# Triangular inverses on all four quarters of TensorE, with operands on swapped halves

## The chip, the cores and the metric

One core of one Trainium2 chip. The metric is device time in microseconds (us) of one execution, median over runs. Engines: PE (TensorE matmul) and PEld (its weight loads), DVE (VectorE), ACT (ScalarE), POOL (GpSimd), SP (SyncE, which issues DMAs here). TensorE's clock is granted at 2.4 GHz (1.00 in the profile) or 1.2 GHz (0.50).

## The reference, cut to what matters

Two stacked models; the change touches only the two chunked scans of the first. The GDN scan solves, per chunk of 64 tokens and head, with a unit lower triangular matrix:

```python
a_mat = jnp.where(strict, bc[..., :, None] * kk * gamma, 0.0) + jnp.eye(C)
u = lax.linalg.triangular_solve(a_mat, bc[..., None] * vc, left_side=True, lower=True)
w = lax.linalg.triangular_solve(a_mat, (bc * jnp.exp(G))[..., None] * kc, left_side=True, lower=True)
...
S = S * jnp.exp(g_last) + einsum(k * jnp.exp(g_last - G), u - w @ S)     # step over 12 chunks
```

The RWKV-7 scan goes token by token, 8 heads of 64, forward and backward; the kernel does it in chunks of 128 tokens:

```python
sa = einsum('bhvk,bhk->bhv', S, -kk_t)
S = S * w_t + sa * (kk_t * a_t) + v_t * k_t
y_t = einsum('bhvk,bhk->bhv', S, r_t)
```

Sequence: 256 context tokens and 512 others, width 1024, all in float32. In both scans the kernel needs the inverse (transposed, TT) of I + A for a strictly triangular 128x128 matrix A per head and chunk of 128.

## The kernel before, in words

The program is 17 stages, one after the other. In each, every engine has its own instruction list, written by generator functions that `in_turn` interleaves round by round; the order on an engine is the order in which the generators yield. Engines wait for each other by semaphores (`wait_ge(*P.at(name))` for the value that `up(name)` gave). There is no planner: the order is fixed by the code.

**PSUM banks.** The eight banks are a ring (`P.bank`, a helper that calls `P.own`): each use takes the next bank and makes PE wait until the bank's previous user is marked "free" (its reader is done). In the GDN scan the ring has 7 banks, since bank 7 belongs to the ada_w products (L551), which run between the scan's own work; in the RWKV scan it has 8.

**The inverse** (`Inverse`, L931 to L1051) works on four heads at once. A 128x128 matrix per head is split in two diagonal 64x64 blocks, one on partitions 0 to 63 and one on 64 to 127, and one off-diagonal block. Tile `TTm` holds `Tm` (the inverse so far) and `TD` (its transpose). ACT copies the diagonal blocks to `AD` and the other to `OFF` (`ac_in`, L1034, L1035). DVE makes `TD = I - AD * mask0` (L990, L992); PE transposes it to PSUM (`Ttr`, L958) and DVE copies that to `Tm` (L995). Then five levels s = 1 to 5 double the size of the solved blocks:

- POOL makes the masked `MT` for the level (L1018, L1023);
- PE: Y = MT by Tm (L949, 8 matmuls of 64x64), ACT copies it to SBUF (L1042);
- PE: the *level product* TY = TD by Y and YT = Y by TD (L949, 16 matmuls), both in one bank;
- DVE subtracts both from TTm in one instruction (L1002), or, at level 5, in three (L1005, two of L1009, which write TT).

At the end Y6 = OFF by Tm (L975), an ACT copy (L1046), U (L981), and an ACT copy into TT (L1049). In every diagonal product the operands and the output lie on the same 64 partitions, so that two of the array's four 64x64 quarters are in use. Each float32 matmul is two records in the trace, one behind the other in PE's list.

**The GDN scan** (`GdnScan`) has six steps, each with both directions d = 0 and 1 side by side. In the rounds of a step PE does: Ttr, WS (L1204), ada_w; Y1, vn (L1212), ada_w; level 1, o (L104) and dS (L1226), ada_w; Y2, qk, ada_w; level 2, gG (L1170); Y3; level 3, gB (L1176); Y4, kk (L1181); level 4; Y5; level 5; Y6; U. The matrix AT of the next step is made by DVE in SBUF during the step. The ada_w weights stream in by DMA, 2 MB at a time into two slots; each is used by two L551 groups.

**The RWKV scan** (`RwkvScan`) has 12 units u, six blocks of 128 tokens forward and six backward; block b is ORDER[u // 6][u % 6], with ORDER = ([0, 1, 2, 3, 4, 5], [1, 0, 5, 4, 3, 2]). Two inverses q = 0, 1 (four heads each) run side by side. PE's order in a unit: AT, BT and, for b >= 2, Qb and Qk (all L1567, two banks each), X of the chain of unit u-1 (L1586, L1589), SA (L1597), Ttr, r_w of the preparation of u+1 (L1723), y of the chain, Y1, r_a (L1728), rS (L104), level 1, and so on; the preparation's transposes (L1736) stand before Y4. DVE's: BT's copy (L1641), TD of both q, the copies of Qb and Qk (L1651), then chain, inverses and preparation in turn. ACT's: AD and OFF of q = 0, AD and OFF of q = 1, X's copy (L1701), SA's copy, and so on.

## Time and profile before

| | us |
|---|---|
| median of 3 runs | 4419.53 |
| lowest, highest run | 4417.85, 4431.77 |
| span of the profiled execution (its own time beside that is not given) | 4426.6 |
| busy in the span: PE, PEld | 3814.4, 2105.2 |
| busy: DVE, POOL, ACT | 2195.7, 1302.2, 878.9 |

The span is from the first to the last instruction. "Busy" is the union of an engine's instructions; matmuls are pipelined and their ends modelled, so PE's busy time is an upper bound of its work. The two scans take 320 us and 535 us of the span. In a timeline row the columns are: start, duration, engine, line, operation, output <- inputs, shapes, count of merged instructions, and in brackets the idle time of the engine before it and what ended it. The duration of a merged row includes the last matmul's pipeline (0.22 us at full clock); how long a row holds the engine is the distance to the next row's start.

### The profile page before, as it was taken

Reading aid. Unit: us, or ns where it says so; the run is one execution under the profiler, and the core shown is the slowest. Engines: PE = TensorE matmul, PEld = TensorE weight load, DVE = VectorE, ACT = ScalarE, POOL = GpSimd, SP = SyncE. Lnnn points to the kernel's source line nnn. Section 1 sums busy time; section 2 is a strip of 40 time slices with the busy share of each in tenths; the row PEclk is TensorE's granted clock in tenths of the full one; section 3 lists DMA queues with packets and bytes.
Section 4 is the critical chain, followed back from the end, with each engine's and each line's share of the span. In section 5 each row is a group of like instructions: output and inputs, shape, how many; then the busy total and the mean of one; then the engine's idle time right before and its main releaser. Section 6 shows DMA issues by size and latency. Waiting matters only on the chain.

```text
span 4426.6 us, 51891 instructions
## 1 busy us (share of the span) xinstructions
PE 3814.4 (86%) x21059; PEld 2105.2 (48%) x21059; DVE 2195.7 (50%) x4428; ACT 878.9 (20%) x1998; POOL 1302.2 (29%) x1372
## 2 busy tenths in 40 slices
PE   7988898888899677777777777779999999989999
PEld 4556665888874322222222222355555444544444
DVE  4845434666544677677577454353332016533320
ACT  1422122333321111111111111221111011521100
POOL 1033301333310277777777777300000000000000
PEclk8999998999899799999999999989999999999999
DMA  4155520000021499999999999711111111012221
GB/s 157 56 190 211 198 70 8 2 2 2 2 73 60 154 409 409 409 409 409 409 409 409 409 400 409 290 35 57 57 39 57 52 50 63 1 39 76 76 71 71
DMA packets 240812, 743.00 MB, mean 168 GB/s; under 512 B 20214, under 2 KB 66561, under 8 KB 231104
## 3 DMA queue, kind: packets, MB, share of 16 engines
q0 software_dynamic: 150992, 549.82, 31.4%
q1 hardware_dynamic: 89008, 187.77, 12.0%
q8 instruction: 168, 2.75, 0.3%
q10 hardware_dynamic: 576, 2.10, 0.1%
q14 instruction: 68, 0.56, 0.0%
HBM read 737.52 MB, written 2.10 MB: 167 GB/s over the span
## 4 chain that ended last, share of the span: by engine, by line
PE 58%; DMA 18%; DVE 13%; POOL 5%; ACT 3%; issue 3%; DVEq 0%; ACTq 0%; POOLq 0%
PE bank L104 34%; DMA wring<-in_peer_down,idxs 11%; PE bank L2466 9%; DMA row<-in_peer_up,idxs 5%; PE bank L949 3%; DVE junk L2375 3%; POOL row L2360 2%; POOL wring L2353 2%; PE bank L2447 2%; DMA wring<-in_ada_w 1%; PE bank L1567 1%; PE bank L551 1%; DVE TTm L1002 1%; DMA row<-in_peer_down,idxs 1%; PE bank L1597 1%
## 5 line engine op out<-in xcount | busy, mean ns | idle before, releaser
L2447 PE MATMUL bank<-row,dg 128*128 128x512 f32 x2048 | 998.3, 618 | 334.3 <-DMA row<-in_peer_up,idxs 214.5
L2447 PEld LDWEIGHTS bank<-row,dg 128*128 128x128 f32 x2048 | 361.6, 193 | 970.6 <-issue 499.4
L104 PE MATMUL bank<-h2T,wring 128*128 128x512 f32 (+1 forms) x2112 | 759.6, 523 | 0.0
L2375 DVE CUSTOM_DVE_ANT_0 junk<-wring,bank 128x1024 f32<-128x1024 f32 x410 | 500.6, 1221 | 328.8 <-DMA wring<-in_peer_down,idxs 307.0
L104 PEld LDWEIGHTS bank<-h2T,wring 128*128 128x128 f32 x2112 | 402.7, 191 | 355.5 <-issue 337.1
L2360 POOL DMA_INDIRECT row<-in_peer_up,idxs x512 | 491.4, 960 | 175.9 <-issue 126.4
L2353 POOL DMA_INDIRECT wring<-in_peer_down,idxs x410 | 391.5, 955 | 146.7 <-issue 83.5
L2466 PE MATMUL bank<-wring,gT 128*128 128x512 f32 x880 | 383.2, 598 | 8.6 <-DVE gT L2864 8.6
L2427 ACT ACTIVATE dg<-consts,cf 128x128 f32<-128x128 f32 x512 | 192.5, 397 | 691.6 <-PE bank L2447 691.3
L2853 DVE TENSOR_SCALAR cv<-pad,fp 128x769 f32<-128x769 f32 (+1 forms) x88 | 54.1, 615 | 509.4 <-ACT pad L2819 509.4
L104 PE MATMUL bank<-hT,wring 128*128 128x256 f32 (+1 forms) x864 | 286.5, 492 | 3.7 <-ACT sq L768 3.0
L2466 PEld LDWEIGHTS bank<-wring,gT 128*128 128x128 f32 x880 | 168.5, 192 | 221.1 <-issue 221.1
L104 PEld LDWEIGHTS bank<-hT,wring 128*128 128x128 f32 x864 | 165.8, 193 | 119.8 <-issue 102.3
L2484 DVE TENSOR_TENSOR tmp<-bank,gr 128x512 f32<-128x512 f32 x28 | 19.3, 691 | 380.8 <-PE bank L2466 345.5
L2900 POOL DMA_DIRECT2D rope<-in_rope x1 | 0.6, 556 | 701.9 <-ACT h2T L2581 701.9
L1023 POOL TENSOR_TENSOR MT<-AD,consts 128x256 f32<-128x256 f32 x144 | 116.1, 825 | 171.8 <-PE bank L949 171.3
L2375 DVE CUSTOM_DVE_ANT_0 junk<-row,bank 128x1024 f32<-128x1024 f32 x102 | 124.5, 1221 | 80.7 <-DMA row<-in_peer_down,idxs 75.3
L104 PE MATMUL bank<-wring,h2T 128*128 128x512 f32 x352 | 156.1, 600 | 3.2 <-ACT h2T L2581 2.3
L949 PE MATMUL bank<-TTm,MT 64*64 64x64 f32 x2880 | 115.6, 227 | 41.2 <-DVE TTm L1002 38.7
L949 PEld LDWEIGHTS bank<-TTm,MT 64*64 64x64 f32 x2880 | 102.0, 139 | 75.2 <-issue 41.2
L1042 ACT ACTIVATE Y<-bank 128x256 f32<-128x256 f32 x180 | 68.2, 382 | 330.7 <-PE bank L949 327.8
L949 PE MATMUL bank<-Y,TTm 64*64 64x64 f32 x2880 | 119.5, 222 | 2.9 <-DVE eG L1256 1.3
(545 smaller groups left out, 4710.9 us busy)
## 6 DMA issues: line engine op xcount, KB each, us to landing
wring<-in_ada_w SPq DMA_DIRECT2D x36, 2048.0 KB, 8.6
wring<-in_ffn_w_up SPq DMA_DIRECT2D x44, 1024.0 KB, 7.7
wring<-in_ffn_w_down SPq DMA_DIRECT2D x8, 2048.0 KB, 8.1
wring<-in_w_in SPq DMA_DIRECT2D x7, 2048.0 KB, 8.2
wring<-in_peer_w_query SPq DMA_DIRECT2D x4, 2048.0 KB, 8.0
row<-in_peer_up,idxs POOLq DMA_INDIRECT x512, 18.2
wring<-in_peer_down,idxs POOLq DMA_INDIRECT x410, 18.0
wring<-in_ffn_w_down SPq DMA_DIRECT2D x4, 1536.0 KB, 6.7
```

Source lines behind the costliest of these rows:

```text
L104: ins = e.matmul(out, l, r, start=(start and n == 0), stop=(stop and n == len(pairs) - 1))
L551: ins = e.matmul(k[32 * j:32 * j + 32, :], P.sc[g // 3 > 0][:, c, :], wb[:, c % 2, j * 512:(j + 1) * 512], start=(c == 0), stop=(c == 7))
L949: ins = e.matmul(k[a, h * 64:(h + 1) * 64], l[a, h, :], r[a, h, :], start=True, stop=True)
L1023: e.tensor_tensor(w["MT"][(s + 1) % 2], w["AD"], self.mask(s + 1), MUL).then_inc(*G.up("MT", u, s + 1))
L1042: e.activation(w["Y"], q4(P.ps("Y", u, s)), ACT.Copy).then_inc(*A.up("free", "Y", u, s))
L2353: e.indirect_dma_start(self.rd[r], None, down, bass.IndirectOffsetOnAxis(ap=idu[:, b, j % 128:j % 128 + 1], axis=0)).then_inc(*self.Ld[r]. ...
L2360: e.indirect_dma_start(self.ru[r], None, up, bass.IndirectOffsetOnAxis(ap=idu[:, b, u % 128:u % 128 + 1], axis=0)).then_inc(*self.Lu[r].up ...
L2375: e.tensor_tensor_reduce(junk, self.rd[j % 10], P.pairs[b % 2], 1.0, 0.0, MUL, ADD, self.dots[:, b % 2, x:x + 1]).then_inc(*V.up("pg_dot", j))
L2427: e.activation(self.dg[u % 4], P.ident, ACT.Copy, scale=self.cf[:, b % 2, x:x + 1]).then_inc(*A.up("pg_scaled", u))
L2447: ins = e.matmul(ks[half], self.dg[u % 4], self.ru[u % 10][:, half * 512:half * 512 + 512], start=(x == 0), stop=(x == 127))
L2466: ins = pe.e.matmul(ks[b], oT[:, k0 + c, off + b * 128:off + (b + 1) * 128], wb[:, c, :], start=(k0 + c == 0), stop=(k0 + c == kc - 1))
L2853: e.tensor_scalar(cc, p[:, s0:s0 + m - 1], w(0), w(3), MUL, ADD).then_inc(*V.up())
```

## The change

- **Banks.** PSUM is declared as four pairs of banks. Each `Inverse` gets a number q and owns pair q: bank A = 2q and bank B = 2q + 1. TY goes to A and YT to B, in columns 0 to 255; Ttr and Y go to B, columns 256 to 511; U goes to A. DVE reads TY and YT in one instruction over both banks (`both`). In the RWKV scan AT goes to A of both inverses as well.
- **The ring** is what is left: banks 4 to 7 in the RWKV scan (ring 4 instead of 8), banks 4 to 6 in the GDN scan (3 instead of 7).
- **Halves.** AD, MT and Tm lie on the other half of the partitions than TD and Y. So Ttr and TY go from rows of one half to columns of the other, Y is made from the swapped halves, and the new `level` function issues TY and YT alternately, so that four matmuls in a row use the four quarters.
- **TD.** DVE reads the source itself instead of AD, in two multiplications of 64 partitions (since the halves are not swapped there), then the subtraction. In the GDN scan the source is AT in SBUF, and DVE waits for AT only; in the RWKV scan it is AT in PSUM, and DVE waits until ACT has made AD.
- **Order.** ACT copies AD of both inverses first and OFF afterwards, once DVE has made TD (`ac_off`). In the RWKV scan DVE makes TD of both inverses before it copies BT.

```diff
-            self.banks = [bank(n, 512) for n in range(4)]
-            self.pairs = [bank(n, 1024) for n in (4, 6)]
-            self.banks += [p[:, s:s + 512] for p in self.pairs for s in (0, 512)]
+            twos = [bank(n, 1024) for n in (0, 2, 4, 6)]
+            self.banks = [p[:, s:s + 512] for p in twos for s in (0, 512)]
+            self.twos = [p.rearrange("p (a i) -> p a i", a=2) for p in twos]
+            self.pairs = twos[2:]
...
-        return self.own(pe, n, *user)
+        return self.own(pe, self.low + n, *user)
...
+    def level(self, pe, u, s):
+        P, e, w = self.P, pe.e, self.w
+        ty, yt = P.own(pe, self.A, "TY", u, s), P.own(pe, self.B, "YT", u, s)
         for h in range(4):
-            for a in (slice(0, 64), slice(64, 128)):
-                ins = e.matmul(k[a, h * 64:(h + 1) * 64], l[a, h, :], r[a, h, :], start=True, stop=True)
-        return ins
+            for a, b in self.halves:
+                e.matmul(ty[b, h * 64:(h + 1) * 64], w["TD"][a, h, :], w["Y"][a, h, :], start=True, stop=True)
+                ins = e.matmul(yt[a, h * 64:(h + 1) * 64], w["Y"][a, h, :], w["TD"][a, h, :], start=True, stop=True)
+        ins.then_inc(*self.st.T.up("TYT", u, s))
...
-            self.pairs(e, k, w["MT"][s % 2], w["Tm"]).then_inc(*T_.up("Yps", u, s))
+            for h in range(4):
+                for a, b in self.halves:
+                    ins = e.matmul(k[a, h * 64:(h + 1) * 64], w["MT"][s % 2][b, h, :], w["Tm"][b, h, :], start=True, stop=True)
+            ins.then_inc(*T_.up("Yps", u, s))
...
-            ins = e.matmul(k[hi, h * 64:(h + 1) * 64], w["OFF"][lo, h, :], w["Tm"][lo, h, :], start=True, stop=True)
+            ins = e.matmul(k[hi, h * 64:(h + 1) * 64], w["OFF"][hi, h, :], w["Tm"][hi, h, :], start=True, stop=True)
...
-        dv.wait_ge(*P.at("AD", u))
+        dv.wait_ge(*P.at(*given))
         if over:
             dv.wait_ge(*P.at(*over))
-        e.tensor_tensor(w["TD"], w["AD"], self.mask(0), MUL).then_inc(*V.up())
+        m0 = self.mask(0)
+        for a, _ in self.halves:
+            e.tensor_tensor(w["TD"][a], src[a, :, a], m0[a], MUL).then_inc(*V.up())
...
-        for a in (slice(0, 64), slice(64, 128)):
-            e.activation(w["AD"][a], src[a, :, a], ACT.Copy).then_inc(*A.up("AD", u))
-        e.activation(w["OFF"][lo], src[lo, :, hi], ACT.Copy).then_inc(*A.up(*free))
+        for a, b in self.halves:
+            e.activation(w["AD"][b], src[a, :, a], ACT.Copy).then_inc(*A.up("AD", u))
+
+    def ac_off(self, ac, u, src, free, over):
+        P, e, w, A, lo, hi = self.P, ac.e, self.w, self.st.A, self.lo, self.hi
+        ac.wait_ge(*P.at("TT", u, 0))
+        if over:
+            ac.wait_ge(*P.at(*over))
+        e.activation(w["OFF"][hi], src[lo, :, hi], ACT.Copy).then_inc(*A.up(*free))
...
 class GdnScan: def pe
-        P.ring = 7
+        P.low, P.ring, P.turn = 4, 3, 0
 class GdnScan: def dv
-            invs = [self.inv[d].dv(dv, (step, d), ("Yps", (step - 1, d), 6) if step else None,
+            invs = [self.inv[d].dv(dv, (step, d), self.W[d]["AT"], ("AT", (step, d)), ("Yps", (step - 1, d), 6) if step else None,
                                    ("vn", (step - 1, d)) if step else None) for d in range(2)]
...
 class RwkvScan: def pe
+        P.low, P.ring, P.turn = 4, 4, 0
...
-                ks = [P.bank(pe, name, u, q) for q in range(2)]
+                ks = [P.own(pe, 2 * q, name, u, q) if name == "AT" else P.bank(pe, name, u, q) for q in range(2)]
 class RwkvScan: def dv
+            invs = [self.inv[u][q].dv(dv, ("r", u, q), v4(P.ps("AT", u, q)), ("AD", ("r", u, q)), ("Yps", ("r", u - 1, q), 6) if u else None,
+                                      ("SA", u - 2) if u >= 2 else None) for q in range(2)]
+            for g in invs:
+                next(g)
             dv.wait_ge(*P.at("BT", u))
             for q in range(2):
                 e.copy_predicated(res[q]["BT"], stri, v4(P.ps("BT", u, q))).then_inc(*V.up("free", "BT", u, q))
             V.mark("free", "BT", u)
-            invs = [self.inv[u][q].dv(dv, ("r", u, q), ("Yps", ("r", u - 1, q), 6) if u else None, ("SA", u - 2) if u >= 2 else None)
-                    for q in range(2)]
-            for g in invs:
-                next(g)
```

## Rows read from the trace of the kernel before

**Rows 1.** The page, the chain that ended last: share of the span by line.
```profile
PE bank L104 34%; DMA wring<-in_peer_down,idxs 11%; PE bank L2466 9%; DMA row<-in_peer_up,idxs 5%; PE bank L949 3%; DVE junk L2375 3%; POOL row L2360 2%; POOL wring L2353 2%; PE bank L2447 2%; DMA wring<-in_ada_w 1%; PE bank L1567 1%; PE bank L551 1%; DVE TTm L1002 1%; DMA row<-in_peer_down,idxs 1%; PE bank L1597 1%
```

**Rows 2.** Busy time by stretch (stretch, length, engines, clock, DMA): the two scans.
```profile
240.00:560.00 320.00, 264.16 (x4284) 193.94 (x4284) 165.56 (x444) 66.06 (x164) 118.96 (x120) 0.94 0.56 209
745.00:1280.00 535.00, 461.37 (x8391) 431.57 (x8390) 312.86 (x515) 179.41 (x380) 168.57 (x171) 0.91 0.01 4
```

**Rows 3.** Timeline of PE: 128x512 on the full array and on four column tiles.
```profile
206.80 13.90 PE L104 MATMUL bank<-wring,hT 128*128 128x512 f32 x32
...
420.69 1.06 PE L551 MATMUL bank<-wring,sc 128*32 128x512 f32 x8
```

**Rows 4.** Timelines of PE, DVE and ACT: end of RWKV unit 4, from level 4.
```profile
912.95 0.68 PE L949 MATMUL bank<-Y,TTm 64*64 64x64 f32 x16
...
914.98 0.68 PE L949 MATMUL bank<-TTm,MT 64*64 64x64 f32 x16
...
916.40 0.66 PE L949 MATMUL bank<-Y,TTm 64*64 64x64 f32 x16
...
918.82 0.68 PE L975 MATMUL bank<-TTm,OFF 64*64 64x64 f32 x8 [0.36 <-DVE TT L1009]
...
921.80 1.16 PE L1567 MATMUL bank<-al,be 64*128 64x128 f32 x16
...
914.14 0.69 DVE L1002 TENSOR_TENSOR TTm<-TTm,bank 128x512 f32<-128x512 f32 x1 [2.25 <-PE bank L949]
915.08 0.69 DVE L1002 TENSOR_TENSOR TTm<-TTm,bank 128x512 f32<-128x512 f32 x1 [0.24 <-PE bank L949]
917.56 0.41 DVE L1005 TENSOR_TENSOR TTm<-TTm,bank 64x256 f32<-64x256 f32 x1 [1.80 <-PE bank L949]
...
918.79 0.41 DVE L1005 TENSOR_TENSOR TTm<-TTm,bank 64x256 f32<-64x256 f32 x1
...
921.90 0.38 ACT L1049 ACTIVATE TT<-bank 64x256 f32<-64x256 f32 x1 [0.36 <-PE bank L981]
```

**Rows 5.** The same timelines: start of RWKV unit 4.
```profile
878.76 1.16 PE L1567 MATMUL bank<-al,be 64*128 64x128 f32 x16
...
881.54 1.06 PE L1567 MATMUL bank<-rho,ka 64*128 64x128 f32 x16
...
880.86 1.35 DVE L1641 COPY_PREDICATED BT<-consts,bank 128x512 f32<-128x512 uint32 x2 [3.91 <-PE bank L1567]
...
882.94 0.83 DVE L992 TENSOR_TENSOR TTm<-consts,TTm 128x256 f32<-128x256 f32 x1
...
885.02 1.33 DVE L1651 COPY_PREDICATED Qb<-consts,bank 128x512 f32<-128x512 uint32 x2
...
879.97 0.78 ACT L1034 ACTIVATE AD<-bank 64x256 f32<-64x256 f32 x2 [0.72 <-PE bank L1567]
```

**Rows 6.** Timelines of PE, DVE and ACT: GDN steps meet; a wait for DMA.
```profile
295.32 1.50 PE L551 MATMUL bank<-wring,sc 128*32 128x512 f32 x8 [2.42 <-DMA wring<-in_ada_w]
...
398.04 0.96 PE L981 MATMUL bank<-TT,Y 64*64 64x64 f32 x16
401.79 2.33 PE L958 MATMUL bank<-consts,TTm 64*64 64x64 f32 x32 [2.79 <-DVE TTm L992]
...
395.95 0.43 DVE L1009 TENSOR_TENSOR TT<-TTm,bank 64x256 f32<-64x256 f32 x1
...
399.56 0.85 ACT L1034 ACTIVATE AD<-AT 64x256 f32<-64x256 f32 x2
```

**Rows 7.** Busy time and granted clock by stretch.
```profile
402.00:408.00 6.00, 5.92 (x52) 5.34 (x54) 1.73 (x4) 0.00 (x0) 2.20 (x3) 0.50 0.47 201
518.00:521.00 3.00, 3.00 (x26) 2.88 (x25) 0.11 (x1) 0.00 (x0) 0.94 (x2) 0.50 0.59 240
437.00:441.00 4.00, 2.14 (x41) 1.97 (x40) 3.59 (x13) 1.07 (x3) 0.00 (x0) 1.00 0.88 369
805.00:818.00 13.00, 13.00 (x108) 11.98 (x109) 4.00 (x7) 3.80 (x6) 3.86 (x4) 0.50 0.00 0
1142.00:1162.00 20.00, 20.00 (x139) 19.08 (x138) 4.48 (x7) 3.90 (x6) 2.79 (x3) 0.51 0.01 2
```

More of the change, by code:

```diff
@@ L211, in __init__ @@
                 self.known, self.value = self.value, {}
[L212 removed]
+                self.holder, self.turn, self.ring, self.low, self.nw = [None] * 8, 0, 8, 0, {"pe": 0, "sy": 0}
                 for s in self.flags:
@@ L994, in dv @@
         dv.wait_ge(*P.at("Ttr", u))
-        e.tensor_copy(w["Tm"], q4(P.ps("Ttr", u))).then_inc(*V.up("free", "Ttr", u))
+        e.tensor_copy(w["Tm"], v4(P.ps("Ttr", u)[:, 256:512])).then_inc(*V.up("free", "Ttr", u))
         yield
@@ L999, in dv @@
             dv.wait_ge(*P.at("TYT", u, s))
[L1000 removed]
+            ps = self.both
             if s < 5:
[L1002 to L1003 removed]
+                tt = w["TTm"].rearrange("p a h i -> p a (h i)")
+                e.tensor_tensor(tt, tt, ps, SUB).then_inc(*V.up("TT", u, s))
             else:
[L1005 removed]
+                e.tensor_tensor(w["Tm"][hi], w["Tm"][hi], v4(ps[:, 0])[hi], SUB).then_inc(*V.up())
                 if over_tt:
                     dv.wait_ge(*P.at(*over_tt))
[L1008 to L1010 removed]
+                for a, _ in self.halves:
+                    e.tensor_tensor(w["TT"][a, :, a], w["TD"][a], v4(ps[:, 1])[a], SUB).then_inc(*V.up("TT", u, s))
+            for x in ("TY", "YT"):
+                V.mark("free", x, u, s)
             yield
@@ L1025, in po, with ac_in @@
             yield
-    def ac_in(self, ac, u, src, given, free, over):
-        P, e, w, A, lo, hi = self.P, ac.e, self.w, self.st.A, self.lo, self.hi
+    def ac_in(self, ac, u, src, given, over):
+        P, e, w, A = self.P, ac.e, self.w, self.st.A
         ac.wait_ge(*P.at(*given))
@@ L1041, in ac @@
             ac.wait_ge(*P.at("Yps", u, s))
-            e.activation(w["Y"], q4(P.ps("Y", u, s)), ACT.Copy).then_inc(*A.up("free", "Y", u, s))
+            e.activation(w["Y"], v4(P.ps("Y", u, s)[:, 256:512]), ACT.Copy).then_inc(*A.up("free", "Y", u, s))
             yield
@@ L1045, in ac @@
         ac.wait_ge(*P.at("Yps", u, 6))
-        e.activation(w["Y"][hi], q4(P.ps("Y", u, 6))[hi], ACT.Copy).then_inc(*A.up("free", "Y", u, 6))
+        e.activation(w["Y"][hi], v4(P.ps("Y", u, 6)[:, 256:512])[hi], ACT.Copy).then_inc(*A.up("free", "Y", u, 6))
         yield
@@ L1075, in __init__ @@
         P.top = top
-        self.inv = [Inverse(self, d, self.W[d]) for d in range(2)]
+        self.inv = [Inverse(self, d, self.W[d], d) for d in range(2)]
         self.og = P.ogdn.rearrange("p b (h e) -> p b h e", h=4)
@@ L1101, in pe @@
         in_turn(*[self.tail_pe(pe, 5, d) for d in range(2)])
-        P.ring = 8
+        P.low, P.ring = 0, 8
     def dv(self, dv):
@@ L1139, in ac @@
                 u = (step, d)
-                self.inv[d].ac_in(ac, u, self.W[d]["AT"], ("AT", u), ("AT_free", u), ("MT", (step - 1, d), 5) if step else None)
+                self.inv[d].ac_in(ac, u, self.W[d]["AT"], ("AT", u), ("MT", (step - 1, d), 5) if step else None)
+            for d in range(2):
+                u = (step, d)
+                self.inv[d].ac_off(ac, u, self.W[d]["AT"], ("AT_free", u), ("Yps", (step - 1, d), 6) if step else None)
             in_turn(*[self.inv[d].ac(ac, (step, d)) for d in range(2)],
@@ L1573, in pe @@
         in_turn(self.chain_pe(pe, 11))
+        P.low, P.ring = 0, 8
     def chain_pe(self, pe, u):
@@ L1689, in ac @@
             for q in range(2):
-                self.inv[u][q].ac_in(ac, ("r", u, q), v4(P.ps("AT", u, q)), ("AT", u), ("free", "AT", u, q),
-                                     ("MT", ("r", u - 1, q), 5) if u else None)
+                self.inv[u][q].ac_in(ac, ("r", u, q), v4(P.ps("AT", u, q)), ("AT", u), ("MT", ("r", u - 1, q), 5) if u else None)
+            for q in range(2):
+                self.inv[u][q].ac_off(ac, ("r", u, q), v4(P.ps("AT", u, q)), ("free", "AT", u, q),
+                                      ("Yps", ("r", u - 1, q), 6) if u else None)
             chain = self.chain_ac(ac, u - 1) if u else iter(())
```

35 lines of the change are left out of this document (13 added, 22 removed).

## The prediction

> **What bounds the kernel now.** I read four views in this order. The chain of waits says who sets the end: TensorE first, DMA second, and the line of the inverses' matmuls (L949) with 3% of the span [rows 1]. The two scans were then cut out by stretches [rows 2]: the GDN scan is 320 us of the span with PE busy 264, the RWKV scan 535 us with PE busy 461. All that the change touches lies in these 855 us, in which no other engine is busy for more than 60% of the time. The timelines of one RWKV unit (u=4) and of one GDN step show what the bound is at each place; in both, PE runs its queue in order and a wait at its head holds everything behind it.
>
> The profiled execution has a span of 4426.6 us; the runs are 4417.85 to 4431.77, median 4419.53, so it is 7.1 us (0.16%) above the median and inside the runs' spread. I work with differences and put them on the median.
>
> **Term 1: the level product.** Per level and inverse, TY and YT are 16 small matmuls, each two records. Before, they run as two groups of 16 records of 0.47 us, 0.93 us together, from the level product's start at 916.40 to DVE's start at 917.56 with 0.25 us of latency [rows 4]. Two tiles already overlap there: 16 records on two tiles show the same 0.68 us as 8 records on one tile in Y6 [rows 4]. Do four quarters overlap four ways? The nearest row is the ada_w matmul, which has four column tiles: 8 records of 128x512 let the next instruction start 0.99 us later, 124 ns each, where a full-array 128x512 takes 13.9/32 = 434 ns [rows 3]. That is 3.5 times, with each matmul's two records next to each other in the queue as here. So I take 0.47 us for a level product; the other end is 0.93, no gain. The Trainium skill ("TensorE: Matmul & The Clock Gate", Part 3, The mechanism) says that a weight load overlaps running matmuls only where the row group differs. Here TY and YT of one half share their rows; by the rule the level product would stay near 0.93 us. The ada_w row disagrees with it, since there all four tiles share every row and still run at once; it keeps a small chance.
>
> **Term 2: RWKV tail of a unit.** Levels 2 and 3 are held by DVE, which has the next unit's preparation between its subtractions; there a faster PE gains nothing. Level 4 on is free of it. Level 4 starts at 912.95 in both versions. With 0.47: the first TTm at 913.67 instead of 914.14; the second inverse's level product waits for its Y copy (913.45), its TTm can start at 914.28 instead of 915.08 (now behind DVE's first, 0.61). Y5 is 0.5 and 0.8 earlier, level 5 starts at 915.69 instead of 916.40, the last subtractions at 916.40 instead of 917.56 and, 1.23 later, 917.63 instead of 918.79 [rows 4]. Y6 follows 1.16 us earlier. Eleven units: -12.8. The last unit has no preparation, so levels 2 to 5 gain some 0.7 us each: -3.0. Sum **-15.8 us**.
>
> **Term 3: AT waits for U's copy.** AT(u+1) now goes into the inverses' own banks A, where U was last. Before, AT starts at 921.80, right behind U; ACT's copy of the second U is 921.90 to 922.28 [rows 4], so AT starts at about 922.4: +0.6 x 11 = **+6.6 us**.
>
> **Term 4: Qk waits for BT in a ring of four.** Banks 4 to 7 now serve everything else. BT takes two, Qb two, and Qk needs BT's two again, so PE stands until DVE has copied BT. And DVE now does the first two TD before BT. From AT's start (878.76 as zero) [rows 5]: ACT starts at 1.2 and needs 0.78 for the first AD pair; the second pair, no longer behind OFF, ends at 2.8. DVE reads the bank from 2.05: two half multiplications (0.41, 0.35 apart) to 2.9, the subtraction 0.83 as beside POOL now, to 3.75; the second inverse the same, to 5.1. BT's copies, 1.35, end at 6.5. Qk starts at 6.6, where it was at 881.54, or 2.8: 3.8 us later. X needs Qb's bank (its copy ends at 7.1) and starts behind Qk. Behind X stand SA, Ttr, r_w, Y1 and r_a, all PE-bound up to DVE's preparation, so nothing absorbs it. Bounds: 3.0 (subtractions at 0.42) to 4.2. It holds for units with b>=2, 8 of 12: **+30.4 us** (24 to 34). In units 1, 6 and 7 only ACT's X copy stands behind the second OFF, which waits for TD: +0.65 x 3 = **+2 us**.
>
> **Term 5: GDN, TD without ACT.** Before, PE stands 2.79 us in front of Ttr at 401.79, for TTm (L992): U's copies, then AD, then two DVE instructions [rows 6]. The source AT is in SBUF and long ready, and DVE is done with the step's last TT at 396.4, so with the new source TD is made while PE still works on Y6 and U. Ttr follows U at once. Such a gap stands in front of steps 1 to 5, 2.7 us each: -13.5; step 0 saves ACT's copies, about 1.2. These gaps also cost clock. After that of 2.79 us the granted clock is 0.50 (1.2 GHz) over 402 to 408, with PE busy 5.92 of 6.0; an idle stretch of 1.86 us at 437 leaves it at 1.00 (2.4 GHz) [rows 7]. Two other steps have the same gap and a shorter half-clock stretch behind it, as over 518 to 521; with theirs I estimate 14 us at half clock, half of it lost: -7. Sum **-22 us** (-12 if the clock stays as it is, -25).
>
> **Term 6: GDN levels.** Levels 1, 2 and 4 are followed at once by work on which the step's chain depends; level 3 is held by DVE (gm, eG), level 5 mostly by the ada_w DMA (a wait as at 295.32) [rows 6]. 0.47 x 2 x 3 in six steps is 17; with two level 5 that are free and some loss to DVE **-17 us** (0 without the four-way overlap, -22 at best). The ring of three costs little here: I followed each use to the one three before it, and only gB of the second direction waits for eG, in a place that DVE holds anyway.
>
> **Term 7: the clock in the RWKV stalls.** Term 4 puts an idle PE of 3.8 us into eight units, longer than the gaps after which the clock fell. And where it falls in front of SA and Ttr it stays down long: PE is busy all of 805 to 818 and of 1142 to 1162 at 0.50 [rows 7]. If a fall follows in 8 of 10 cases and lasts 10 us with PE on the path for most of it, half is lost at worst: I take 4 us x 6.5 = **+26 us** (0 to +70).
>
> The other edits cost nothing on the path: in the GDN scan DVE's second multiplication lies in its idle time behind U, OFF's later copy has until Y6, the swap of halves in AD and MT changes only addresses, and Y6 and U, which share rows now, may lose 0.2 us where they interleave.
>
> **Sum.** -15.8 + 6.6 + 30.4 + 2 - 22 - 17 + 26 = +10.2 us: 4430 us.
>
> **The rivals.**
> - *The clock holds* (or recovers within X). For it: X and Qk are matmuls over whole rows, and most of the scan runs at 1.00. Against: the falls after the gaps of 2.4 and 2.8 us. Then term 7 is zero: -16 us, 4404 us. Faster.
> - *The clock stays down through the small matmuls*, as it did over 1142 to 1162: 8 x 8 us instead of 26 in all: 4419.5 - 16 + 64 = 4468 us. Slower. It decides once a fall outlasts X, because the work behind (SA, Ttr, r_w, Y1) keeps PE busy and still did not bring the clock back in those two stretches.
> - *The quarters overlap only in pairs.* Then terms 2 and 6 vanish, the waits remain: +43 us, 4462 us. Against it stands the ada_w row. It would also hold if the change did not do what its words say.
>
> **How the numbers follow.** Forecast 0.38 (its own range 4412 to 4448), clock holds 0.30, clock stays down 0.17, pairs only 0.15. A measurement of this kernel tells about 0.3% (13 us) from no change. Slower by more: 0.45 of the forecast case, and both slow rivals, 0.17 + 0.32 = 0.49. Faster by more: two thirds of the clock-holds case and a little of the forecast, 0.23. The rest, 0.28, is within. Range 4396 to 4470.
>
> **What the profile after would show.** Level products with TY and YT mixed, 32 records in about 0.5 us, against 0.93: term 1. PE waiting 3.5 to 4 us for DVE's BT in front of Qk in units 2 to 5 and 8 to 11, and unit starts there 3 us further apart (term 4 and 3 less term 2); no wait for L992 in front of Ttr in the GDN scan, and that scan 35 to 40 us shorter; the granted clock over 745 to 1280 below the 0.91 of now. Wrong would be: no wait in front of Qk, level products of 0.9 us, or a GDN scan that is no shorter because DMA takes back what PE gains.

## The result: 1.8% slower, and where the time went

The changed kernel takes 4506.35 us (median of 4 runs, 4499.31 to 4510.58) against 4425.65 us of the kernel before beside it (4 runs, 4417.85 to 4435.38): ratio 1.0181, 95% interval 1.0153 to 1.021. Its profiled execution has a span of 4508.0 us, 81.4 more than that of before. The forecast was 4430, the range ended at 4470: the sign of the likeliest single outcome (slower, 0.49) was right, the size was not.

Cut at the first AT of the RWKV scan and at the AT of its last unit, the two kernels stand so (stretch, length, busy time of PE, its weight loads, DVE, ACT, POOL with counts, granted clock, DMA share, GB/s). Before:

```profile
240.80:758.90 518.10, 448.42 (x5008) 310.47 (x5008) 250.16 (x566) 111.11 (x267) 126.86 (x128) 0.94 0.39 143
758.90:1228.80 469.90, 411.62 (x7595) 384.29 (x7594) 284.94 (x470) 163.69 (x347) 154.75 (x155) 0.92 0.01 2
```

After:

```profile
240.80:738.90 498.10, 429.38 (x5010) 284.97 (x5010) 255.69 (x578) 111.81 (x267) 123.64 (x128) 0.92 0.40 149
738.90:1293.10 554.20, 450.44 (x7593) 414.50 (x7593) 293.46 (x492) 166.52 (x348) 151.92 (x155) 0.74 0.01 2
```

Up to the RWKV scan the change gains 20.0 us. The eleven units then lose 84.3, and the last unit with what follows 17.1: together +81.4. The clock of the RWKV scan went from 0.92 to 0.74. The part of the stretch in which PE isn't busy grew from 58.3 to 103.8 us, by 45.5; busy time grew by 38.8, although the level products should have taken some 0.46 x 2 x 5 x 11 = 51 us out of it. So about 90 us are matmuls that ran at half clock (38.8 + 51, an estimate): twice what the longer waits cost. The clocks give the same size: (1 - 0.74) x 2 x 554.2 = 288 us were granted at 0.50, against 75 before, and a busy engine loses half of such time.

The 45.5 us can be read from PE's waits in these stretches (line <- what it waited for: us in total, times, longest). In the changed kernel L955 is TY, L956 YT, L974 Y, L983 Y6, L989 U, L965 Ttr, L1589 AT, BT, Qb and Qk, L1620 SA and L1761 the preparation's transposes. After:

```profile
PE bank L974 <- DVE TTm L1013: 32.9, 27, 2.3
PE bank L1589 <- DVE BT L1668: 19.0, 7, 3.4
PE bank L983 <- DVE TT L1019: 13.9, 22, 0.9
PE bank L1761 <- DVE rho L1808: 12.9, 8, 2.0
...
PE bank L1589 <- ACT TT L1067: 5.6, 10, 0.6
```

Before:

```profile
PE bank L949 <- DVE TTm L1002: 21.9, 33, 1.7
PE bank L975 <- DVE TT L1009: 10.8, 22, 0.6
PE bank L1736 <- DVE rho L1783: 8.3, 8, 1.0
```

Qk's wait for BT (19.0) and AT's for U's copy (5.6) are new. The rest is longer waits for TTm, rho and TT, behind the shorter level products. I read it as the level products' own gain given back, where DVE holds the level.

The timeline of PE and DVE at the start of unit 3 (start, duration, instruction, idle before it and who ended it) answers to [rows 5]:

```profile
877.73 1.68 PE L1589 MATMUL bank<-rho,be 64*128 64x128 f32 x16
882.03 1.77 PE L1589 MATMUL bank<-rho,ka 64*128 64x128 f32 x16 [2.62 <-DVE BT L1668]
...
877.12 0.87 DVE L1000 TENSOR_TENSOR TTm<-bank,consts 64x256 f32<-64x256 f32 x2 [5.80 <-ACT AD L1045]
...
879.91 0.60 DVE L1002 TENSOR_TENSOR TTm<-consts,TTm 128x256 f32<-128x256 f32 x1
880.55 1.33 DVE L1668 COPY_PREDICATED BT<-consts,bank 128x512 f32<-128x512 uint32 x2
```

The order is the predicted one: TD twice, then BT, and Qk behind it. Qb took 1.68 us instead of 1.06 (its row at 880.64 in the trace of before): the clock is already down when the unit starts. So Qk comes 7.85 us after AT (874.18), where 2.78 was the time before and 6.6 the forecast. Four of the stretches at half clock, by place: in Qk and X of unit 3, between its levels, at its end, and in unit 2 behind the wait:

```profile
882.40:885.80 3.40, 3.40 (x25) 3.18 (x22) 2.07 (x5) 0.00 (x0) 0.00 (x0) 0.50 0.00 0
909.80:916.50 6.70, 5.55 (x106) 5.03 (x107) 4.21 (x7) 1.84 (x4) 3.03 (x3) 0.50 0.01 2
923.50:930.10 6.60, 5.91 (x53) 5.65 (x54) 1.70 (x3) 2.45 (x7) 1.64 (x3) 0.50 0.01 4
827.90:851.60 23.70, 22.92 (x202) 21.51 (x203) 6.95 (x13) 4.39 (x7) 4.98 (x5) 0.50 0.00 1
```

Units 3, 4 and 5 have the first three at the same distances from AT (8.2, 35.5 and 49.2 us) and take 51 us each instead of 43. In units 2, 8, 9 and 10 the stretch at 6.5 to 8.4 us lasts 24 to 34 us; they take 54.7 to 63.2 us instead of 38 to 54.

Which units get a long stretch changes from one execution to the next. The old RWKV scan stands in five traces (the kernel before, e4, e8, e15 and e16 below); each has one or two stretches of 20.5 us in units with b>=2, in unit 9, in 3, in 4 and 9, in 4 and in 9. A trace shows one execution, so its list of stretches is a sample, and the ratios over all runs decide.

The level product itself did what was forecast. The first two and the last record of one inverse's 32, and the first of the other's (unit 3, level 2):

```profile
905.03 0.27 PE L955 MATMUL bank<-Y,TTm 64*64 64x64 f32 x1
905.04 0.27 PE L956 MATMUL bank<-TTm,Y 64*64 64x64 f32 x1
...
905.51 0.22 PE L956 MATMUL bank<-TTm,Y 64*64 64x64 f32 x1
905.63 0.27 PE L955 MATMUL bank<-Y,TTm 64*64 64x64 f32 x1
```

### The profile page after: what moved, and what is told of

The parts are those of the page before. It is cut to its first block, busy times and chain, and to the rows that moved or that the text cites. A ratio compares the mean times of both kernels' runs of the same rounds, so it can differ in the third digit from the quotient of the medians.

```text
span 4508.0 us, 51934 instructions
## 1 busy us (share of the span) xinstructions
PE 3852.0 (85%) x21059; PEld 2122.6 (47%) x21059; DVE 2209.0 (49%) x4464; ACT 882.1 (20%) x1998; POOL 1295.4 (29%) x1372
## 4 chain that ended last, share of the span: by engine, by line
PE 50%; DMA 16%; DVE 12%; POOL 5%; issue 3%; ACT 3%; DVEq 0%; ACTq 0%; POOLq 0%
PE bank L104 29%; DMA wring<-in_peer_down,idxs 10%; PE bank L2491 8%; DMA row<-in_peer_up,idxs 4%; DVE junk L2400 3%; POOL row L2385 3%; DMA row<-in_peer_down,idxs 2%; POOL wring L2378 2%; PE bank L2472 2%; PE bank L974 1%; PE bank L1589 1%; PE bank L1620 1%; PE bank L1612 1%; DVE TTm L1013 1%; POOL row L2378 1%
## 5 line engine op out<-in xcount | busy, mean ns | idle before, releaser
L974 PE MATMUL bank<-TTm,MT 64*64 64x64 f32 x2880 | 127.1, 244 | 56.3 <-DVE TTm L1013 53.5
L974 PEld LDWEIGHTS bank<-TTm,MT 64*64 64x64 f32 x2880 | 110.7, 154 | 94.6 <-DVE TTm L1013 79.0
L955 PE MATMUL bank<-Y,TTm 64*64 64x64 f32 x2880 | 118.9, 235 | 2.2 <-ACT Y L1060 2.0
```

Source lines behind the costliest of these rows:

```text
L955: e.matmul(ty[b, h * 64:(h + 1) * 64], w["TD"][a, h, :], w["Y"][a, h, :], start=True, stop=True)
L974: ins = e.matmul(k[a, h * 64:(h + 1) * 64], w["MT"][s % 2][b, h, :], w["Tm"][b, h, :], start=True, stop=True)
```

## Experiments

Each ran beside the kernel before; the ratio is to that. From e5 to e12 a later part of the program, which nothing here touches, had a lower granted clock (tenths by slice, page of e9_at_in_b and below it of e16_gdn_only_again), and the kernel before took 4571 to 4574 us instead of 4426 to 4430. That part is full of DMA (busy nine tenths and more), which moved 350 to 372 GB/s in e9 and 405 to 409 in e16. So ratios are compared, not times.

```profile
PEclk8989897777789788788878888889999999999999
```

```profile
PEclk8989898999889799999999999989999999999999
```

"Scan" is the stretch from the first AT to that of the last unit in the profiled execution: its length, PE's busy time in it, its granted clock. The profiled execution can lie off the median: for e3 (4477 us, median 4460), e7 (4615, 4593) and e2 (4526, 4515) it is the slowest of the runs, for e17 (4437, 4455), e15 (4423, 4435) and e1 (4526, 4534) the fastest.

| kernel | ratio, 95% interval | scan us | PE busy | clock |
|---|---|---|---|---|
| before | 1 | 469.9 | 411.6 | 0.92 |
| changed | 1.0181 (1.0153-1.021) | 554.2 | 450.4 | 0.74 |
| e1_bt_first | 1.0226 (1.0189-1.0264) | 572.2 | 461.7 | 0.73 |
| e2_two_groups | 1.0171 (1.0134-1.0208) | 576.5 | 475.1 | 0.75 |
| e3_qb_twice | 1.006 (1.0037-1.0084) | 524.6 | 424.8 | 0.80 |
| e4_gdn_only | 0.9929 (0.99-0.9959) | 468.6 | 410.1 | 0.92 |
| e5_qk_in_b | 1.008 (1.005-1.0109) | 528.1 | 434.7 | 0.76 |
| e6_qk_in_b_pairs | 1.0078 (1.0057-1.01) | 514.1 | 425.7 | 0.83 |
| e7_levels_again | 1.0052 (1.0035-1.0069) | 523.3 | 450.9 | 0.80 |
| e8_gdn_pairs | 0.996 (0.9938-0.9981) | 475.4 | 417.4 | 0.90 |
| e9_at_in_b | 1.0067 (1.0048-1.0087) | 520.6 | 437.1 | 0.75 |
| e10_at_in_b_again | 1.0014 (0.9992-1.0036) | 493.4 | 427.0 | 0.84 |
| e11_levels_twice | 1.0282 (1.0259-1.0306) | 611.7 | 515.4 | 0.75 |
| e12_before_u_wait | 1.0043 (1.0022-1.0065) | 503.8 | 439.6 | 0.86 |
| e13_before_bt_wait | 1.0219 (1.0181-1.0258) | 557.3 | 480.2 | 0.79 |
| e14_changed_filled | 1.0069 (1.0042-1.0095) | 521.3 | 435.4 | 0.85 |
| e15_gdn_levels_twice | 1.0016 (0.9995-1.0038) | 464.7 | 406.6 | 0.93 |
| e16_gdn_only_again | 0.9954 (0.993-0.9979) | 469.2 | 409.9 | 0.92 |
| e17_before_bt_wait_filled | 1.0072 (1.0037-1.0108) | 482.4 | 416.4 | 0.94 |

### The scans apart

e4_gdn_only: `RwkvScan` and the inverse it uses are those of before, `GdnScan` that of the change.

> The GDN scan as in the changed kernel, the RWKV scan as in the kernel before. In the changed kernel's trace the RWKV scan starts 20 us earlier than before and runs some 100 us longer. Theory: the two scans do not act on each other, so the GDN scan's 20 us remain: 4406 us against 4426 of before. Rival: the earlier start shifts the weight loads and clock of what follows, and the gain is taken back there: 4420 to 4430 us.

The gain of the GDN scan stays whole. The loss of the changed kernel is all in the RWKV scan, some 100 to 110 us (1.0181 less 0.9954 of e16, the same kernel again, or less 0.9929, of 4426), and this version is faster than both kernels.

### The wait in the changed kernel

e1_bt_first:

```diff
-            invs = [...]; for g in invs: next(g)      # TD of both inverses
             dv.wait_ge(*P.at("BT", u))
             ... copies of BT ...
+            invs = [...]; for g in invs: next(g)
```

> DVE copies BT out of its banks before it makes TD, in the RWKV scan; all else as in the changed kernel. In the changed kernel's trace, PE stands 2.6 us in front of Qk in the eight units with b>=2, and a half-clock stretch begins 8.2 us into each; others begin 35.5 and 49.2 us into it, behind gaps of 1.5 to 2.0 us between levels. Theory: two independent triggers, the wait for BT and the gaps that the shorter level products leave. Then this takes away 2.6 x 8 = 21 us of waiting and some 4 us of half-clock loss per unit between AT and SA (33), and leaves the other stretches: about 4452 us. Rival 'stall alone' (the later stretches only follow from the first): the whole clock loss of some 100 us goes, 4400 to 4410 us. Rival 'levels alone': only the waiting goes, 4485 us, and half-clock time in the RWKV scan stays above 300 us.

All expectations missed: it is no faster. Its timeline of PE (unit 5) shows why; the wait only moved from Qk to X, whose bank of the ring of four was Qb's:

```profile
1004.68 1.16 PE L1589 MATMUL bank<-rho,ka 64*128 64x128 f32 x16 [0.25 <-DVE BT L1664]
1007.92 0.49 PE L1609 MATMUL bank<-S,al 128*128 128x128 f32 x2 [2.08 <-DVE Qb L1674]
```

e3_qb_twice:

```diff
-                for x in range(4):
+                for x in (0, 1, 2, 3) * (2 if name == "Qb" else 1):
```

> The Qb product of the RWKV scan is issued twice, the second time with the same operands into the same banks, so that PE works 0.9 us (full clock) to 1.7 us (half clock) of the 2.6 us that it would wait for BT. More work, same chain. Theory (both triggers): the stretch at +8.2 us goes in most units, -4 us each, and the work itself is hidden: about 4475 us. Rival 'stall alone': 4415 us. Rival 'it is the waits, not the clock': 4506 us or above, up to +8 us where the extra work is not hidden.

Work without use made the kernel 1.2% faster (1.0181 to 1.006, 4506 to 4460 us). The length of the waits can't explain it: in the profiled executions the waits for BT fell only from 19.0 to 14.0 us. It speaks for the clock. In the seven units with b>=2 of the scan, half-clock time between 6 us after AT and 17 us before the next went from 127 to 25 us, while that of the last 17 us stayed (48 and 43). A second trigger was left. Two long stretches are in its trace instead of four: 20.5 us in unit 5, from 14.9 us on, and 37 us from the start of unit 6, which has no Qk and had no such stretch in the changed kernel. The idle time alone doesn't sort the units. In 3, 8 and 9 PE still stands 2.4 to 2.6 us in front of Qk, as long as in the changed kernel, and no long stretch follows; the work in front of the wait is what differs there. Unit 8, the row of Qk and the stretch from it on, at full clock:

```profile
1131.10 1.16 PE L1589 MATMUL bank<-rho,ka 64*128 64x128 f32 x16 [2.57 <-DVE BT L1668]
```

```profile
1130.00:1156.00 26.00, 18.44 (x410) 16.96 (x411) 17.95 (x29) 8.66 (x17) 8.43 (x8) 1.00 0.01 2
```

### The level products

e2_two_groups and e6_qk_in_b_pairs (e5's edit with this one in the RWKV scan), e8_gdn_pairs (e4's edit with this one):

```diff
         for h in range(4):
             for a, b in self.halves:
                 e.matmul(ty[b, ...], w["TD"][a, h, :], w["Y"][a, h, :], ...)
+        for h in range(4):
+            for a, b in self.halves:
                 ins = e.matmul(yt[a, ...], w["Y"][a, h, :], w["TD"][a, h, :], ...)
```

> The level product is issued as 16 records of TY and then 16 of YT, so that only two quarters run at once; banks, waits and all else as in the changed kernel. Theory (both triggers): level products go from 0.47 back to 0.93 us, which costs up to 33 us on the path, and the gaps between levels shrink to 0.7 and 1.25 us, which takes the stretches at +35.5 and +49.2 us away and gives back some 3 to 4 us per unit: about 4495 us, with the stretch at +8.2 still there. Rival 'stall alone': 4506 + 33 = 4539 us. Rival 'levels alone': 4506 - 100 + 33 = 4440 us. If four quarters never overlapped more than pairs, no change at all: 4506 us with unchanged level products.

> As e4_gdn_only (RWKV scan as before the change), with the level products of the GDN scan in two groups. What is left of the change is TD read straight from AT, the banks, and OFF's later copy. My term for the four-quarter levels in this scan was -17 us and for the early TD -22 us; e4 measured -28 in all. Theory: both terms were too large by the same share: 4398 + 12 = 4410 us. Rival 'DVE and the clock hold the levels': 4398 us, all of the gain is TD's. Rival 'levels are the whole gain': 4426 us.

Neither result tells the theories apart, since the edit does only half of what I meant. TY (L955) and YT (L958) of e2_two_groups still run at once for the greater part; the timeline of PE shows TY ten records ahead and then both in turn:

```profile
1030.64 0.51 PE L955 MATMUL bank<-Y,TTm 64*64 64x64 f32 x10
1030.93 0.27 PE L958 MATMUL bank<-TTm,Y 64*64 64x64 f32 x2
1030.98 0.28 PE L955 MATMUL bank<-Y,TTm 64*64 64x64 f32 x3
1031.04 0.22 PE L958 MATMUL bank<-TTm,Y 64*64 64x64 f32 x1
```

At full clock the 64 records of both inverses start within 1.35 us (median), against 0.94 where nothing else holds them in the changed kernel and 1.86 before. So about half of the gain comes from where operands and banks lie, and the rest from the order in the queue. The Trainium skill ("TensorE: Matmul & The Clock Gate", Part 3, The mechanism) names a reorder window of TensorE in which weight loads for another part of the array go ahead of running matmuls. That work for different parts overlaps, these traces bear out. By the same section loads do so only where the row group differs, and there the traces disagree: TY and YT of one half share their rows, and in the changed kernel they start 0.01 us apart (905.03 and 905.04 above). It also keeps the matmuls themselves in the order of the program, and this trace disagrees: YT starts at 1030.93, ahead of the last six records of the same inverse's TY, which stand before it in the queue.

e11_levels_twice:

```diff
-        for h in range(4):
+        for h in list(range(4)) * (2 if u[0] == "r" else 1):
```

> The changed kernel with each level product of the RWKV scan issued twice (same operands, same banks), so that it takes the 0.93 us of before again while all waits and banks stay as changed. (Two groups in the queue did not do this: in their trace the records of TY and YT still alternate, 64 of them in 1.1 us.) Theory: the gaps of 1.5 and 2.0 us between levels shrink to those of before and with them the half-clock stretches at +35 and +49 us; the product costs 16 us on the tail; net 0 to 20 us faster than the changed kernel's 1.0181: 1.014. Rival 'shorter level products do not touch the clock': 16 to 25 us slower, 1.022 or above. Rival 'they alone hold it down': 1.000.

45 us slower than the changed kernel by the ratios, more than any theory gave. The half-clock time in the last 17 us of those seven units did go, from 48 to 4 us, but that between 6 us after AT and 17 us before the next grew from 127 to 212: each of the seven units now has one stretch of 20 to 34 us, from 6 to 9 us on. So the levels' length acts on the clock at a unit's end. Why the stretches behind the wait grew, with much the same waiting in front of them (22.0 us in seven units against 19.0), isn't shown.

### Without the bank waits

e5_qk_in_b and e9_at_in_b, both with e1's edit:

```diff
-  ks = [P.own(pe, 2 * q, name, u, q) if name == "AT" else P.bank(pe, name, u, q) ...]
+  ks = [P.own(pe, 2 * q + (name == "Qk"), ...) if name in ("AT", "Qk") else P.bank(...) ...]   # e5
+  ks = [P.own(pe, 2 * q + (name == "AT"), ...) if name in ("AT", "Qk") else P.bank(...) ...]   # e9
```

> The changed kernel with DVE's BT copies ahead of TD and, besides, the Qk product in the inverses' own banks B instead of the ring of four, so that neither Qk nor X stands behind a copy of Q (with BT first alone, the 2.1 us wait had only moved from Qk to X). Four-quarter levels stay in both scans. Theory: the wait in the unit's head is the main trigger of half clock, the gaps that the short level products leave a lesser one. Then the head of a unit takes as long as before the change, the tail keeps a stretch of some 7 us at half clock in part of the units: 4405 to 4420 us. Rival 'head alone': the clock is back throughout, and the levels' 16 us less the 7 us of AT behind U's copy show: 4390 us, below the 4398 of the kernel with the old RWKV scan. Rival 'levels alone': clock time stays, about 4480 us.

> As e5_qk_in_b with the two banks swapped: AT goes into the inverses' banks B (last held by Y6, whose copy ends before U's), Qk into their banks A. So none of AT, Qk and X waits for a bank; BT first on DVE, four-quarter levels in both scans. Given as a ratio to the kernel before, since chips differ: e5 had 1.008. Theory: each wait that the change adds around the small matmuls of a unit's tail and head lowers the granted clock of the work behind it. Then AT's wait of 0.56 us behind U is worth more than its 0.56 x 11 = 6 us: with some 2 us of clock a unit, 30 us in all, ratio 1.001. Rival 'AT's wait is worth itself': 1.0065. Rival 'the short level products alone hold the clock down': 1.0065 here too, and e11_levels_twice shows it.

With no wait for Qk or X, e5 takes back more than half of the change's loss (1.0181 to 1.008). Taking AT's wait away as well gave what the wait itself costs or nothing (1.008 and 1.0067, the intervals overlap). The scan of e9 stays 51 us longer than before, at a clock of 0.75.

One kind of wait is left in both, and it is the change's. In the units without Qb and Qk, SA waits for ACT's copy of X, which stands in ACT's queue behind the OFF copies, and those wait for TD. Here TD is behind BT, so they come late. Timeline of PE, unit 1 of the kernel before and of e9:

```profile
803.42 2.82 PE L1597 MATMUL bank<-X,TT 128*128 128x64 f32 x16 [0.69 <-ACT X L1701]
```

```profile
786.14 3.68 PE L1620 MATMUL bank<-X,TT 128*128 128x64 f32 x16 [3.20 <-ACT X L1726]
```

In units 6 and 7 the same wait is 1.46 and 1.53 us in e9, against 0.69, and unit 6 takes 51.2 us instead of 41.0; behind its wait PE is busy at half clock:

```profile
1030.00:1057.30 27.30, 25.80 (x296) 24.51 (x296) 9.12 (x13) 6.26 (x10) 6.89 (x6) 0.50 0.00 1
```

e7_levels_again adds to e5, and e10_at_in_b_again to e9:

```diff
+        again = {1: 1, 2: 2, 3: 2}.get(s, 0) if u[0] == "r" and u[2] == 1 else 0
-        for h in range(4):
+        for h in list(range(4)) * (1 + again):
```

> As e5_qk_in_b, but the second inverse's level product of levels 1, 2 and 3 of the RWKV scan is issued again (once, twice, twice; same operands, same banks), in the time in which DVE is still at the next unit's preparation. It is work without use, 0.5 to 0.9 us each. Theory: it keeps PE busy in the gaps of 1.5 and 2.0 us, so half-clock time falls and the kernel is 5 to 20 us faster than e5. Rival 'gaps do not touch the clock': the same as e5 or up to 5 us slower.

> As e9_at_in_b, with the second inverse's level product of levels 1, 2 and 3 in the RWKV scan issued again (once, twice, twice) while DVE is at the preparation. The same addition took e5 from 1.008 to 1.0052. Theory: here it is worth as much, 10 us: ratio 0.999. Rival 'the gaps no longer matter once the tail has no wait': the same as e9, or 0.001 above.

e10 is 0.5% faster than e9 with more work and the intervals apart; the clock of its scan rose from 0.75 to 0.84. For e7 against e5 (0.3%) the intervals overlap. e6, in which the level products take 0.68 us, came out as e5:

> As e5_qk_in_b, with the level product of the RWKV scan in two groups (TY, then YT), as it was before the change; the GDN scan keeps four quarters. Theory: the gaps between levels are those of before (0.7 and 1.25 us), the half-clock stretches in the tail go, and the rest costs 0.6 us a unit: 4398 + 7 = 4405 us, no slower than e5. Rival 'the levels do not touch the clock': e5 + 16 us. Rival 'levels alone': 4405 us while e5 stands at 4480.

e14_changed_filled puts e3's and e7's fillings into the changed kernel:

> The changed kernel with both fillings and nothing else: Qb issued twice (alone: 1.006) and the second inverse's level products 1, 2 and 3 of the RWKV scan issued again (alone, in two other kernels: 0.003 and 0.005 faster). Theory: the two kinds of gap cost clock in different parts of the unit, so the gains add up: 1.002. Rival 'the levels' gaps matter only once the head has no wait': 1.006.

1.0069, as e3 alone: the fillings did not add up where the wait for BT is still there.

### The waits alone, in the kernel before

e12_before_u_wait and e13_before_bt_wait are the kernel before with an edit; e17_before_bt_wait_filled is e13 with Qb issued three times:

```diff
+            for q in range(2 if u else 0):                     # e12
+                pe.wait_ge(*P.at("free", "U", ("r", u - 1, q)))
             for name, l, r in (...):
+                if name == "Qk":                               # e13, e17
+                    pe.wait_ge(*P.at("free", "BT", u))
-                for x in range(4):
+                for x in (0, 1, 2, 3) * (3 if name == "Qb" else 1):   # e17
...
+            for g in invs: next(g)                             # e13, e17: TD ahead of BT
             ... copies of BT ...
```

> The kernel before with one wait more: AT of a unit of the RWKV scan waits for the copy of the unit before's U, as it does in the changed kernel. Nothing else is changed. Theory: 0.56 us x 11 of waiting and some 1 to 2 us of half-clock loss a unit in front of and behind AT: 15 to 25 us, ratio 1.0045. Rival 'a wait is worth itself': 6 us, ratio 1.0015.

> The kernel before with the wait in front of Qk alone: DVE makes TD before it copies BT, and PE waits for BT's copies in front of Qk, as in the changed kernel; banks, halves and level products are those of before. By ACT's and DVE's durations Qk starts some 3 us later in 8 units: 25 us of waiting. Theory: this wait alone takes the clock down for most of the stretch up to the levels, so 40 to 60 us more: ratio 1.017. Rival 'a wait is worth itself': 1.0055. Rival 'only together with the short level products': 1.006 to 1.009.

> As e13_before_bt_wait (kernel before, DVE's TD ahead of BT, Qk waits for BT's copies; ratio 1.0219), with the Qb product issued three times instead of once, so that PE works some 1.8 us of the 3.2 us in front of Qk. Theory: the time beyond the waiting itself (25 of 100 us) is the clock's, called down by PE's idling; with the gap down to 1.4 us most of it comes back: ratio 1.008. Rival 'DVE's order costs the time': the same 1.022 or, where the extra matmuls aren't hidden, above.

These show that the wait is enough. e13 is above even the theory's 1.017. Nothing of the quarters or banks is in it, only the wait and DVE's order (TD ahead of BT), and a loss of the same size is there: 1.0219, and the scan 87.4 us longer. 18.8 of these are time in which PE isn't busy (557.3 - 480.2 against 58.3); 68.6 are busy time of the same instructions. They don't show that the wait is all of the changed kernel's loss: with it gone, e5 and e9 keep 1.008 and 1.0067, and the gain of the GDN scan is in these. One wait of e13 and what follows, timeline of PE, unit 9:

```profile
1200.11 2.08 PE L1569 MATMUL bank<-rho,ka 64*128 64x128 f32 x16 [3.60 <-DVE BT L1647]
1202.12 0.79 PE L1588 MATMUL bank<-S,al 128*128 128x128 f32 x2
...
1208.28 3.65 PE L1599 MATMUL bank<-X,TT 128*128 128x64 f32 x16 [0.78 <-ACT X L1703]
1211.85 1.97 PE L958 MATMUL bank<-consts,TTm 64*64 64x64 f32 x32
```

By stretch, PE is busy all but 0.8 of 28 us behind it and stays at half clock:

```profile
1202.00:1230.00 28.00, 27.22 (x169) 26.03 (x168) 5.08 (x10) 4.50 (x7) 1.53 (x3) 0.50 0.00 1
```

In e17, with the same wait and DVE's order, PE idles 1.14 us instead of 3.2 in unit 4:

```profile
925.56 2.84 PE L1569 MATMUL bank<-rho,be 64*128 64x128 f32 x48
929.54 1.16 PE L1569 MATMUL bank<-rho,ka 64*128 64x128 f32 x16 [1.14 <-DVE BT L1647]
```

In its profiled execution, the fastest of seven, the scan has no stretch at half clock behind the wait in any unit with b>=2; by the ratio over all seven runs two thirds of the loss are gone. The order on DVE is that of e13, so it isn't the order that costs the time. Unit 4 of e13 is the one of its seven units in which no long stretch follows the wait, of 3.23 us; in its unit 5 one of 30.7 us follows a wait of 1.99.

e12's 0.56 us waits cost 19 us by the ratio (10 to 29 by its interval) where 6 would be their length; PE's busy time rose by 28 us in its profiled execution. In the changed kernel the same wait is worth less or nothing, as e9 against e5 says: the prices of the waits don't add up.

### The GDN scan taken apart

e15_gdn_levels_twice is e4 with `for h in list(range(4)) * 2` in the level product; e16_gdn_only_again is e4.

> GDN scan of the changed kernel with each level product issued twice (0.93 us again), RWKV scan of before. Against e16_gdn_only_again on the same chip. My term for the four-quarter levels in the GDN scan was 17 us, for the early TD 22. If both hold in proportion: 0.003 above e16. Rival 'TD alone': the same as e16. Rival 'levels alone': back at 1.000.

> The same kernel as e4_gdn_only (GDN scan changed, RWKV scan of before), run again beside e15_gdn_levels_twice as its reference and as the version that is faster than both kernels: 0.993 as it measured, 0.996 as its two-group variant did.

The four-quarter levels are worth 24 us (4435.2 against 4410.9), and with level products of the old length the early TD leaves nothing (1.0016, not told from 1). Stretch from the scan's start to the first AT, e15 and e16:

```profile
239.30:764.00 524.70, 452.18 (x6930) 309.09 (x6930) 255.59 (x578) 111.81 (x267) 124.02 (x128) 0.94 0.39 142
```

```profile
241.20:738.20 497.00, 429.68 (x5010) 285.27 (x5010) 254.82 (x578) 111.89 (x267) 123.64 (x128) 0.92 0.41 149
```

Why the early TD gives so little is in DVE's timeline of the changed kernel, and PE's below it, where steps 1 and 2 meet:

```profile
342.91 0.69 DVE L575 COPY mr<-bank 128x512 f32<-128x512 f32 x1 [6.54 <-PE bank L552]
343.63 0.87 DVE L1000 TENSOR_TENSOR TTm<-AT,consts 64x256 f32<-64x256 f32 x2
344.53 0.43 DVE L1002 TENSOR_TENSOR TTm<-consts,TTm 128x256 f32<-128x256 f32 x1
344.88 1.36 DVE L1000 TENSOR_TENSOR TTm<-AT,consts 64x256 f32<-64x256 f32 x2
346.27 0.84 DVE L1002 TENSOR_TENSOR TTm<-consts,TTm 128x256 f32<-128x256 f32 x1
...
345.01 0.68 PE L965 MATMUL bank<-consts,TTm 64*64 64x64 f32 x16 [1.14 <-DVE TTm L1002]
347.17 1.12 PE L965 MATMUL bank<-consts,TTm 64*64 64x64 f32 x16 [1.47 <-DVE TTm L1002]
```

DVE stands 6.5 us in front of the copy of an ada_w product (L575), which is queued ahead of TD and waits for a PE matmul that PE reaches only between Y6 and U. In steps 2 and 5 the early TD comes as late as the old one; in 1, 3 and 4 the gap in front of Ttr is gone. Step 0 got longer: PE reaches its first gG product at 265.05 instead of 259.83, in the trace of the changed kernel. There the two half multiplications of TD, while POOL works too, take up DVE for 1.33 and 2.89 us where 0.42 and 0.41 did:

```profile
254.09 1.33 DVE L1000 TENSOR_TENSOR TTm<-AT,consts 64x256 f32<-64x256 f32 x2
...
256.21 2.89 DVE L1000 TENSOR_TENSOR TTm<-AT,consts 64x256 f32<-64x256 f32 x2
```

## Why the prediction failed, term by term

- **Term 1, the level product, right.** 32 records of one inverse start within 0.48 us, the next inverse's 0.60 after the first; 0.47 was forecast.
- **Term 2, the tail, right in shape.** From level 4 to Y6 unit 4 takes 4.90 us against 5.87 (912.95 to 918.82 in [rows 4]), 0.97 of the 1.16 forecast. Its price over the whole scan wasn't measured by itself.
- **Term 3, AT behind U's copy, right in length, not in price.** 0.56 us, ten times in the stretch. I left it without a clock price; e12 puts 19 us on the same wait in the kernel before, e9 against e5 next to none in the changed one.
- **Term 4, Qk behind BT, right in kind.** 19.0 us in seven units, 2.7 each, where 3.8 was forecast. The wait is shorter because AT, BT and Qb in front of it ran at half clock; Qk itself came 5.1 us later than before, counted from AT. Of the +2 us for units 1, 6 and 7 only 0.8 came, in unit 7.
- **Term 5, the early TD, wrong:** -22 forecast, nothing to be told from zero measured. The step that failed is "with the new source TD is made while PE still works on Y6 and U": I looked at when DVE was done with TT and not at what stands between TT and TD in its queue. PE's idle time in front of Ttr fell from 23.3 to 12.7 us over the six steps, and step 0 gives 5.2 us of that back, with multiplications of which a pair cost up to seven times the one that it replaces. The clock's share of the term, -7, failed too: the granted clock up to the RWKV scan fell from 0.94 to 0.92, so that some 80 us were at half clock instead of 60, and it was 0.94 in e15 with the long level products.
- **Term 6, the GDN levels, too small:** -17 forecast, -24 measured. With term 5 the scan gained 20 us, where the sum had 39.
- **Term 7, the clock, is the error that matters.** +26, at most 70, was forecast; about 90 us is what the trace gives, and e13 shows 69 us from the BT wait, in a kernel that has nothing else of the change but DVE's order. Two steps failed. First, "lasts 10 us": in four of the seven units with b>=2 it lasts 24 to 34 us. The rows for that were in my hands [rows 7], 13 and 20 us at 0.50 with PE busy throughout; I took less than either. Second, I gave a clock price to the 3.8 us wait alone. Gaps of half a microsecond at the unit's end (e12) and of 1.5 to 2 us between the shortened levels (e10 against e9) can have one too.

The rival "the clock stays down through the small matmuls" had the right mechanism and priced it at 64 us; with 90 instead of 64, and a GDN scan that gained 20 instead of 39 us, it gives 4513. The 90 is read from the result, so that 4513 lies close to it is no test. "Pairs only" is refuted by the level products, "the clock holds" by 0.74.

Open stays what keeps the clock down once it has fallen: in units 3 to 5 of the changed kernel the stretch behind the wait is 3.4 us long, in units 2 and 8 to 10 it is 24 to 34, with the same instructions. The length of the wait doesn't settle it: 2.55 to 2.63 us are followed by 3.4 us in three units and by 24 to 31 in three others, and 2.4 to 2.6 by none in e3. Open too is why e10, without any bank wait and with its gaps half filled, is still 0.6 to 0.9% behind the version with the old RWKV scan. The late copy of X may be a part of it: units 1, 6 and 7 of e10, where SA waits 1.5 to 3.1 us for it, are 13 us longer together than in the kernel before; no run tests that by itself. And it is open why the fillings help in e10 and not in e14.

## What to carry to other kernels

Before TensorE's queue gets a new wait, look at what stands behind it and price that work at half clock for as long as the worst stretch in the trace, not the mean one. Even half a microsecond can cost three times its length (e12). A faster product in front of a wait for another engine is not a gain but a gap; it can be filled with work without use to see whether the clock is the cost (e3: 47 us faster for more work). Judge that by many runs, since one trace shows one execution's stretches. And before calling an operation "free early", read the whole queue of its engine between the last use and the new place.

## What the runs showed of the hardware that was not expected

- Matmuls on different quarters overlap even where they are issued in groups: the 32 matmuls of TY and YT (64 records) of two inverses started within 1.35 us, as against 0.94 us in turn and 1.86 us on two quarters (e2_two_groups, the changed kernel, the kernel before). The expectation of e11 has 1.1 us for the first of these; the trace has 1.35.
- A clock that has fallen in or behind a wait of 2.0 to 3.6 us can stay at 0.50 for 20 to 34 us, with PE busy 27.22 of 28 us (e13). It doesn't always: 3.23 us in unit 4 of e13 had no such stretch behind it, nor had 2.4 to 2.6 us in three units of e3. Waits of at most 1.8 us in the same place had none in the trace of e17 (7.4 us in six units); in e3 one of 20.5 us began 7 us behind a wait of 1.80.
- The kernel before took 4426 us at one time and 4571 us at another on one chip. At the slower time a part of the program that is full of DMA moved 350 to 372 GB/s instead of 405 to 409 (e9, e16), and its granted clock was 0.8 instead of 0.9; which of the two brings the other isn't shown.
